# Moving the whole first map of a convolution module ahead of the depthwise convolution, and issuing the first loads from two engines

## The chip, the core and the metric

The kernel runs on one core of one Trainium2 chip. The metric is the device time of one execution in microseconds (us); three executions of the kernel before gave 954.35, 954.5 and 955.32 us, median 954.5 us. Work is shared by TensorE (PE, matrix multiplies into PSUM banks), VectorE (DVE), ScalarE (ACT), GpSimd (POOL) and SyncE (SP, which issues loads). The engines run their own instruction streams in order and wait for each other by semaphores.

## The reference

Two layers over 512 tokens of 1024 channels, float32. Only the first layer's token mixer is touched by the change:

```python
h = rmsnorm(x, norm_mix[0])
a = h @ w_pw1 + b_pw1                      # 1024 -> 2048
u = a[..., :d] * sigmoid(a[..., d:])       # gated: 1024 channels
u = causal_dwconv(u, w_dw, b_dw)           # 31 taps for each channel
u = silu(layernorm(u, ln_g, ln_b))
x = x + (u @ w_pw2 + b_pw2)
```

After it come a ConvFFN (up projection 1024 -> 5632, a convolution of width 3, gating, down projection), a pooling mixer, a second ConvFFN and a final RMSNorm.

## The kernel before, in words

Channels lie on the 128 partitions, in 8 tiles of 128 channels; tokens (512) lie along the free dimension. Each float32 operand is split in a rounded part (`_hi`) and a rest (`_lo`), and each product takes three matmul passes: hi by hi, lo by hi and hi by lo. A weight block of 128x2048 ("unit") is loaded to `w_raw[s]` by SP, rounded to `w_hi[s]` by ACT (`round_unit`, L451; the second unit of all at L492) and its rest made in `w_lo[s]` by DVE or POOL (`split_unit` L753, `split` L362). There are two slots, s = 0 and 1.

**The first map** (`w_pw1`) has four steps i = 0 to 3. Step i makes output tiles 2i and 2i+1: unit s = 0 their value half, unit s = 1 their gate half, 48 matmuls of 128x512 each. `first_unit` (L1210 to L1220) is step 0's value unit; it takes its weights in four parts and the input chunk by chunk as they land. The sum over channels for the RMSNorm (`sum_channels(0)`, L1136) is placed inside step 0's gate unit. It waits for `sumsq`: ACT squares each input tile (L470) and DVE adds them (L797). ACT takes the root (L464), DVE its reciprocal in `rms` (L772), and the results of the map are scaled by `rms` as they are drained (`scale_val` L853, `drain_gate` L859); ACT makes the sigmoid (L540), DVE multiplies value and gate (`multiply` L871).

**The depthwise convolution** is shared out. DVE makes four of the eight tiles (two pairs, `SUM_PAIRS`): per tile 31 taps, each one instruction over 512 tokens (`taps`, L841). PE makes the other four (`CONV_TILES`), each in two `conv_unit`s for 64 channels: 16 shifts by three passes of 128x256, 48 matmuls (L1165 to L1167). A conv unit's weights are blocks built from the taps, the hi block by ACT (`build_hi` L532) or POOL and the lo block by POOL (`build` L375); blocks are put in places that become free as the map ends. Its input is the gated map, rounded and rearranged by ACT (`round_even` L548, `cross_even` L555) and split by POOL (`split_even` L371). Tile 6 is shared: its first 3 shifts (6 taps) are DVE's (`shared_tap` L903, L907), and PE leaves these matmuls out. ACT drains a finished conv tile with four instructions (`drain_conv` L564).

The order is written out by hand in each engine's program. On PE it is: map steps 0, 1 and 2, conv units 0 and 1 (tile 2), map step 3, conv unit 2, a matmul for an early estimate of the channel mean (`sum_near` L1240), conv units 3 to 7. Conv unit 7 waits until tile 6 (units 4 and 5) is drained by ACT (`even_drained` at 12), since it writes the same bank. Inside unit 7, after 42 matmuls, PE makes a matmul on `rest_sum` (`sum_rest`, L1248), which DVE sums after its last tap (L923 to L934). POOL subtracts the estimated mean from the four finished tiles (L422), and ACT squares them (L603) before it drains tile 6. Then come the LayerNorm's statistics, and the second map.

**The first loads** are all issued by SP, in this order: small parameters, input tile 0, part 0 of the first unit, tile 1, tiles 2-3, part 1, tiles 4-5, parts 2 and 3, tiles 6-7, the second unit (1 MB, L320), taps, identity. An input tile is 0.25 MB (all of x 2 MB), a part 0.25 MB.

Of the kernel before, what the change touches and what calls it, by code (L numbers as in the profile page):

```python
# [81 lines left out]
CONV_TILES, SUM_PAIRS = (2, 3, 6, 7), (0, 2)  # L82
# [7 lines left out]
BUILT_BY_ACT, BUILT_BY_POOL = (0, 1, 4, 5, 7), (2, 3, 6)  # L90
# [5 lines left out]
NEAR_TILES = (0, 1, 2)  # L96
NEAR_SCALE = KD / len(NEAR_TILES)
SHARED_TILE, SHARED_SHIFTS = 6, 3
# [7 lines left out]
BANKS_PW1 = [(0, 2), (6, 0), (2, 6), (2, 6)]  # L106

BANKS_CONV = (0, 0, 1, 1, 0, 0, 1, 0)
# [6 lines left out]
def build(nc, x_in, vecs, ident_in, band_in, w_pw1, w_pw2, w_up, w_down, w_pool, out):  # L115
# [5 lines left out]
    with ctx:  # L121
# [62 lines left out]
        conv_hi = [block_hi[0], block_hi[1], block_hi[0], block_hi[1], block_hi[2], w_hi[0], w_hi[1], block_hi[3]]  # L184
        conv_lo = [block_lo[0], block_lo[1], block_lo[0], block_lo[1], block_lo[2], w_lo[0], w_lo[1], block_lo[3]]
# [38 lines left out]
        x_loaded = sems("x_loaded", 5)  # L224
# [8 lines left out]
        squared, summed = sem("squared"), sem("summed")  # L233
        stat_mm, root_done, rms_ready = sem("stat_mm"), sem("root_done"), sem("rms_ready")
# [60 lines left out]
        def _(sp):  # L295
# [30 lines left out]
            sp.wait_ge(conv_done, 5)  # L326
# [21 lines left out]
        def _(pool):  # L348
# [38 lines left out]
            pool.wait_ge(w_split[1], M_PW1 + 3)  # L387
# [3 lines left out]
            split(0, M_PW1 + 3)  # L391
            split(1, M_PW1 + 3)
            for u in (2, 3):
                pool.wait_ge(conv_done, u - 1)
                build(conv_hi, tap_hi, u).then_inc(hi_by_pool, 1)
                build(conv_lo, tap_lo, u).then_inc(lo_built, 1)
            pool.wait_ge(w_split[1], M_PW1 + PW1_STEPS)
            build(conv_lo, tap_lo, 4).then_inc(lo_built, 1)
            pool.wait_ge(unit_done[0], M_PW1 + PW1_STEPS)
            build(conv_lo, tap_lo, 5).then_inc(lo_built, 1)  # L400

# [15 lines left out]

# [3 lines left out]
            for c in range(4):  # L421
                nc.gpsimd.tensor_tensor(conv_out[:, c, :], conv_out[:, c, :], near_mean, SUB).then_inc(dev_early, 1)  # L422
# [23 lines left out]
        def _(act):  # L446
# [42 lines left out]
            square_in(0)  # L489
# [1013 lines left out]
```

## Time and profile before

| | |
|---|---|
| Times of three executions | 954.35, 954.5, 955.32 us (median 954.5) |
| The profiled execution's own time | 956.41 us |
| Its span, first to last instruction | 954.6 us |
| PE busy | 941.1 us, 99% |
| DVE, ACT, POOL busy | 555.8, 387.6, 112.2 us |
| Mean granted TensorE clock | 0.991 |

The profiled execution took 1.8 us outside its span, and 1.9 us more than the median of the runs. A PE that is shown busy may still run at half the clock, so the granted clock is read beside it. In the 40 slices of the page, PE is at nine tenths or more in all but the first and the last; DVE is as full as PE only in the first six slices (up to 143 us), where the convolution is.

### The profile page before, as it was taken

The page shows a single profiled execution, that of the slowest core. Times are in us where ns is not written, and L with a number is a line of the kernel's source. Part 1 is how long each engine was busy: PE and PEld are TensorE (multiplying, and loading weights), DVE is VectorE, ACT ScalarE, POOL GpSimd, SP SyncE. Part 2 cuts the span into 40 slices and gives each one's busy share as a digit, 9 for nine tenths or more (in the row PEclk, how much of TensorE's full clock was granted, in tenths as well). Part 3 has the DMA queues.
Part 4 walks back from the last instruction along what each step waited for, and adds up shares of the span by engine and source line. Part 5 has one row for each costly group of instructions (what it writes and reads, how often), then busy time and mean ns, then how long its engine had stood idle before and what let it go on. Part 6 is the DMA issues. An engine that isn't in the chain of part 4 may idle for free.

```text
span 954.6 us, 11837 instructions
## 1 busy us (share of the span) xinstructions
PE 941.1 (99%) x4476; PEld 791.3 (83%) x4476; DVE 555.8 (58%) x712; ACT 387.6 (41%) x593; POOL 112.2 (12%) x73
## 2 busy tenths in 40 slices
PE   8999999999999999999999999999999999999996
PEld 6889898888888888888888898888888888888886
DVE  6899995557655555555434359765555555532333
ACT  7785696344333333333223355433333333321220
POOL 0558796000000000000000020000000000000000
PEclk9999998999999999999999999999999999999998
DMA  7320022222332222322232331233222232223212
GB/s 256 111 89 1 1 90 89 89 89 88 107 114 88 88 88 88 100 92 76 78 119 91 117 134 66 89 107 113 88 88 88 88 102 91 75 90 108 91 61 88
DMA packets 17019, 88.55 MB, mean 93 GB/s; under 512 B 2016, under 2 KB 4320, under 8 KB 9952
## 3 DMA queue, kind: packets, MB, share of 16 engines
q1 hardware_dynamic: 16416, 87.67, 26.9%
q10 hardware_dynamic: 576, 0.52, 0.2%
q8 instruction: 16, 0.26, 0.1%
q14 instruction: 11, 0.09, 0.0%
HBM read 86.09 MB, written 2.10 MB: 92 GB/s over the span
## 4 chain that ended last, share of the span: by engine, by line
PE 94%; DVE 4%; DMA 1%; issue 0%; ACT 0%; SPq 0%; DVEq 0%
PE bank L1114 29%; PE bank L1116 29%; PE bank L1115 29%; DVE bank L841 2%; PE bank L1428 1%; DMA x_res<-x 1%; PE bank L1176 1%; DVE out_sb L1104 1%; PE bank L1182 0%; PE bank L1165 0%; PE bank L1166 0%; PE bank L1167 0%; PE bank L1396 0%; PE bank L1400 0%; PE bank L1401 0%
## 5 line engine op out<-in xcount | busy, mean ns | idle before, releaser
L1114 PE MATMUL bank<-h_hi,w_hi 128*128 128x512 f32 x800 | 312.3, 390 | 0.0
L1116 PE MATMUL bank<-h_hi,w_lo 128*128 128x512 f32 x800 | 311.3, 389 | 0.0
L1115 PE MATMUL bank<-h_lo,w_hi 128*128 128x512 f32 x800 | 311.2, 389 | 0.0
L451 ACT ACTIVATE w_hi<-w_raw 128x2048 fp32r<-128x2048 f32 (+2 forms) x87 | 147.3, 1693 | 211.9 <-PE bank L1116 211.8
L753 DVE TENSOR_TENSOR w_lo<-w_raw,w_hi 128x2048 fp32r<-128x2048 f32 (+2 forms) x81 | 162.2, 2002 | 100.5 <-ACT w_hi L451 99.8
L1114 PEld LDWEIGHTS bank<-h_hi,w_hi 128*128 128x128 f32 x800 | 150.2, 188 | 31.6 <-issue 0.5
L1115 PEld LDWEIGHTS bank<-h_lo,w_hi 128*128 128x128 f32 x800 | 150.2, 188 | 31.4 <-issue 0.5
L1116 PEld LDWEIGHTS bank<-h_hi,w_lo 128*128 128x128 f32 x800 | 150.2, 188 | 31.4
L1115 PE MATMUL bank<-u_lo,w_hi 128*128 128x512 f32 (+1 forms) x422 | 159.5, 378 | 0.0
L1114 PE MATMUL bank<-u_hi,w_hi 128*128 128x512 f32 (+1 forms) x374 | 141.1, 377 | 0.4 <-DVE w_lo L753 0.4
L1116 PE MATMUL bank<-u_hi,w_lo 128*128 128x512 f32 (+1 forms) x374 | 140.8, 376 | 0.0
L1115 PEld LDWEIGHTS bank<-u_lo,w_hi 128*128 128x128 f32 x422 | 79.4, 188 | 14.8
L1114 PEld LDWEIGHTS bank<-u_hi,w_hi 128*128 128x128 f32 x374 | 70.4, 188 | 13.4 <-DVE w_lo L753 0.6
L993 DVE TENSOR_TENSOR act_in<-bank,rms 128x512 f32<-128x512 f32 x44 | 28.4, 687 | 90.9 <-PE bank L1116 87.7
L1116 PEld LDWEIGHTS bank<-u_hi,w_lo 128*128 128x128 f32 x374 | 70.4, 188 | 13.0
L841 DVE SCALAR_TENSOR_TENSOR bank<-glu,par,bank 128x512 f32<-128x512 f32 x116 | 77.8, 748 | 0.0
L457 ACT ACTIVATE sq<-x_res 128x512 f32 (+1 forms) x23 | 14.5, 630 | 128.4 <-DVE x_res L1020 105.2
L666 ACT ACTIVATE u_hi<-y 128x512 f32 (+1 forms) x44 | 27.1, 633 | 89.2 <-DVE y L1008 89.2
L1008 DVE TENSOR_TENSOR y<-bank,y 128x512 f32<-128x512 f32 x44 | 28.4, 686 | 55.6 <-PE bank L1116 55.6
L662 ACT ACTIVATE y<-y 128x512 f32<-128x512 f32 x44 | 27.9, 633 | 58.4 <-DVE y L1001 57.8
L436 POOL TENSOR_TENSOR up_lo<-w_raw,up_hi 128x2048 fp32r<-128x2048 f32 x1 | 4.6, 4644 | 398.3 <-ACT up_hi L690 398.3
L1020 DVE TENSOR_TENSOR x_res<-bank,x_res 128x512 f32 (+1 forms) x15 | 10.4, 692 | 68.3 <-PE bank L1116 68.3
(195 smaller groups left out, 988.0 us busy)
## 6 DMA issues: line engine op xcount, KB each, us to landing
w_raw<-w_up SPq DMA_DIRECT2D x44, 1024.0 KB, 4.8
w_raw<-w_down SPq DMA_DIRECT2D x32, 704.0 KB, 4.1
w_raw<-w_pw SPq DMA_DIRECT2D x11, 1024.0 KB, 5.0
x_res<-x SPq DMA_DIRECT2D x3, 512.0 KB, 8.0
out<-out_sb SPq DMA_DIRECT2D x12, 128.0 KB, 1.8
w_raw<-w_pw SPq DMA_DIRECT2D x4, 256.0 KB, 7.7
w_raw<-w_pool SPq DMA_DIRECT2D x2, 512.0 KB, 3.8
band_raw<-band SPq DMA_DIRECT2D x1, 800.0 KB, 6.4
```

The source lines that it names most:

```text
L451: nc.scalar.activation(w_hi[s][:, 0:columns], w_raw[s][:, 0:columns], ACT.Copy).then_inc(w_rounded[s], 1)
L457: nc.scalar.activation(sq[:, t, :], chunk(x_res, c), ACT.Square).then_inc(squared, 1)
L662: nc.scalar.activation(y[:, t, :], y[:, t, :], ACT.Silu).then_inc(silu_done[t], 1)
L666: nc.scalar.activation(chunk(u_hi, 2 * i + t), y[:, t, :], ACT.Copy).then_inc(u_rounded[t], 1)
L753: V.tensor_tensor(w_lo[s][:, 0:columns], w_raw[s][:, 0:columns], as_f32(w_hi[s][:, 0:columns]), SUB).then_inc(w_split[s], 1)
L841: V.scalar_tensor_tensor(acc if k < TAPS - 1 else conv_out[:, c, :], src, w, acc, MUL, ADD).then_inc(tap_step[t], 1)
L993: V.tensor_tensor(act_in[:, t, 2:2 + T], bank[t][:, :], rms[:, :], MUL).then_inc(drained[t], 1)
L1008: V.tensor_tensor(y[:, t, :], bank[2 + t][:, :], y[:, t, :], MUL).then_inc(drained[2 + t], 1)
L1020: V.tensor_tensor(chunk(x_res, e), bank[t][:, :], chunk(x_res, e), ADD).then_inc(x_updated, 1)
L1114: M.matmul(dst, a, hi, start=start, stop=False)
L1115: M.matmul(dst, a, lo, start=False, stop=False)
L1116: return M.matmul(dst, b, hi, start=False, stop=stop)
```

## The change

Five things change.

1. **Order on PE.** All four steps of the map stand ahead of all conv units. DVE's four convolution tiles are now 0 to 3 (map steps 0 and 1), PE's are 4 to 7 (steps 2 and 3). Blocks, banks and the orders of ACT and POOL follow. The early mean is taken over tiles 0, 1 and 4. Tile 6 is still the shared one, with 4 shifts (8 taps) on DVE in place of 3.
2. **Step 0's gate unit** is a function of its own (`second_unit`): it starts when `w_hi[1]` is rounded, takes the passes that need only that first, and those with `w_lo[1]` later, in two groups of rows.
3. **The sum of squares** is placed after 22 of its matmuls in place of 30. ACT makes all eight squares behind the rounding of the second unit, and DVE adds them as a tree of five instructions, two of them over 1024 elements, with no cleared start.
4. **First loads.** SP issues parameters, then all of x in six loads, then the second unit. ACT issues the four parts of the first unit: two ahead of its first work, each of the others after a part is rounded.
5. **Small moves.** The pooling vectors go from DVE (after the reciprocal) to POOL (at the start); the sigmoid's table is loaded ahead of `tap_columns`, and the first sigmoid stands ahead of a rounding; the wait for the second map's loads is `conv_done` 3 in place of 5.

The first place is PE at the end of step 0's value unit and in its gate unit, before (`w_hi_69` and `w_lo_71` are the gate unit's weights; between the pieces the three passes repeat):

```order
L1220 MATMUL bank<-h_hi,w_lo_70 128x512 x2
L1114 MATMUL bank<-h_hi,w_hi_69 128x512 [waits w_split1]
L1115 MATMUL bank<-h_lo,w_hi_69 128x512
L1116 MATMUL bank<-h_hi,w_lo_71 128x512
...
L1136 MATMUL bank<-sumsq,ones 128x512 [waits summed]
L1114 MATMUL bank<-h_hi,w_hi_69 128x512
```

and now:

```order
L1228 MATMUL bank<-h_hi,w_lo_70 128x512 x2
L1239 MATMUL bank<-h_hi,w_hi_69 128x512 [waits w_rounded1]
L1240 MATMUL bank<-h_lo,w_hi_69 128x512
...
L1246 MATMUL bank<-h_hi,w_lo_71 128x512 [waits w_split1]
L1246 MATMUL bank<-h_hi,w_lo_71 128x512 x5
L1239 MATMUL bank<-h_hi,w_hi_69 128x512
...
L1141 MATMUL bank<-sumsq,ones 128x512 [waits summed]
L1239 MATMUL bank<-h_hi,w_hi_69 128x512
```

The unit no longer waits for the rest of its weights at its start, and the matmul on `sumsq` stands eight places earlier.

The second place is ACT at the same time. Before:

```order
L481 ACTIVATE w_hi_68<-w_raw_66 128x512 [waits raw_loaded0]
L475 ACTIVATE h_hi<-x_res,par 128x512 [waits x_loaded4] x2
L470 ACTIVATE in_sq<-x_res 128x512 x2
L492 ACTIVATE w_hi_69<-w_raw_67 128x2048 [waits raw_loaded1]
L470 ACTIVATE in_sq<-x_res 128x512 x6
L451 ACTIVATE w_hi_68<-w_raw_66 128x2048 [waits unit_done0,raw_loaded0]
```

and now:

```order
L467 DMA w_raw_66<-w_pw 128x512
L480 ACTIVATE h_hi<-x_res,par 128x512 [waits x_loaded3]
L480 ACTIVATE h_hi<-x_res,par 128x512 [waits x_loaded4]
L486 ACTIVATE w_hi_68<-w_raw_66 128x512 [waits part_loaded2]
L480 ACTIVATE h_hi<-x_res,par 128x512 [waits x_loaded4]
L486 ACTIVATE w_hi_68<-w_raw_66 128x512 [waits raw_loaded0]
L480 ACTIVATE h_hi<-x_res,par 128x512 [waits x_loaded5] x2
L497 ACTIVATE w_hi_69<-w_raw_67 128x2048 [waits raw_loaded1]
L475 ACTIVATE in_sq<-x_res 128x512 x8
L450 ACTIVATE w_hi_68<-w_raw_66 128x2048 [waits unit_done0,raw_loaded0]
```

All eight squares now stand behind the rounding of the gate unit's weights.

The third place is POOL from the second half of the conv inputs on (`block_hi0` and `w_hi1` are places of conv blocks, `sq` holds the near sum). Before:

```order
L371 TENSOR_TENSOR even_lo_81<-glu_even_79,even_hi_80 64x2x271 x4
L375 TENSOR_TENSOR w_hi1_69<-pair_mask_94,tap_hi_92 128x2048
L375 TENSOR_TENSOR block_lo3_89<-pair_mask_94,tap_lo_93 128x2048
L422 TENSOR_TENSOR conv_out_77<-conv_out_77,sq_74 128x512 x4
L427 TENSOR_TENSOR dev_sq_96<-dev_sq_96 128x512 x3
```

and now:

```order
L369 TENSOR_TENSOR even_lo_81<-glu_even_79,even_hi_80 64x2x271 x4
L408 TENSOR_TENSOR sq_74<-sq_74,conv_out_77 128x512
L373 TENSOR_TENSOR block_hi3_85<-pair_mask_94,tap_hi_92 128x2048
L373 TENSOR_TENSOR block_hi0_82<-pair_mask_94,tap_hi_92 128x2048
L373 TENSOR_TENSOR block_lo0_86<-pair_mask_94,tap_lo_93 128x2048
L373 TENSOR_TENSOR block_lo1_87<-pair_mask_94,tap_lo_93 128x2048
L421 TENSOR_TENSOR conv_out_77<-conv_out_77,sq_74 128x512 x4
L426 TENSOR_TENSOR dev_sq_96<-dev_sq_96 128x512 x3
```

Four builds and an addition stand between the last split of a conv input and the subtractions, in place of two builds.

The diff, cut to what the order doesn't tell:

```diff
-CONV_TILES, SUM_PAIRS = (2, 3, 6, 7), (0, 2)
+CONV_TILES, SUM_PAIRS = (4, 5, 6, 7), (0, 1)
-BUILT_BY_ACT, BUILT_BY_POOL = (0, 1, 4, 5, 7), (2, 3, 6)
+BUILT_BY_ACT, BUILT_BY_POOL = (0, 1, 2, 4, 7), (3, 5, 6)
-NEAR_TILES = (0, 1, 2)
+NEAR_TILES = (0, 1, 4)
-SHARED_TILE, SHARED_SHIFTS = 6, 3
+SHARED_TILE, SHARED_SHIFTS = 6, 4
-BANKS_CONV = (0, 0, 1, 1, 0, 0, 1, 0)
+BANKS_CONV = (6, 6, 1, 1, 0, 0, 1, 0)
 ...  # SP
-            load_x(0, 0, 1)
-            load_part(0)
-            load_x(1, 1, 2)
-            load_x(2, 2, 4)
-            load_part(1)
-            load_x(3, 4, 6)
-            load_part(2)
-            load_part(3)
-            load_x(4, 6, 8)
+            for c in range(4):
+                load_x(c, c, c + 1)
+            load_x(4, 4, 6)
+            load_x(5, 6, 8)
 ...  # ACT
+            load_part(0)
             act.wait_ge(consts_set, CONSTS)
             nc.scalar.activation(warm[:, :], eps[:, 0:1], ACT.Copy)
+            load_part(1)
 ...
                 round_part(n)
+                if n + 2 < PARTS:
+                    load_part(n + 2)
 ...  # DVE
+            def add_squares(n):
+                dve.wait_ge(squared, Q_IN + 4 * n + 4)
+                V.tensor_tensor(in_sq[:, 4 * n:4 * n + 2, :], in_sq[:, 4 * n:4 * n + 2, :], in_sq[:, 4 * n + 2:4 * n + 4, :], ADD).then_inc(in_added, 1)
+                dve.wait_ge(in_added, 2 * n + 1)
+                V.tensor_tensor(in_sq[:, 4 * n, :], in_sq[:, 4 * n, :], in_sq[:, 4 * n + 1, :], ADD).then_inc(in_added, 1)
 ...
             split_unit(1, M_PW1, UNIT)
-            for c in range(2, KD):
-                add_square(c)
+            add_squares(0)
+            add_squares(1)
+            dve.wait_ge(in_added, 4)
+            V.tensor_tensor(sumsq[:, :], in_sq[:, 0, :], in_sq[:, 4, :], ADD).then_inc(summed, KD + 1)
 ...  # PE, conv_unit
-                if n < 2:
-                    wait_drained((2, 3), DRAINED_PW1 + 2)
+                if n == 0:
+                    wait_drained((2, 3), DRAINED_PW1 + 3)
+                elif n < 3:
+                    for t in range(2):
+                        pe.wait_ge(glu_done[t], PW1_STEPS)
                 else:
-                    pe.wait_ge(even_drained, 12 if u == CONV_UNITS - 1 else 4 * (n - 2) + 4)
+                    pe.wait_ge(even_drained, 8 if g == 0 else 12)
 ...  # PE
+            def second_unit():
+                pe.wait_ge(w_rounded[1], 1)
+                for rows in ((0, 1, 2), (3, 4, 5, 6, 7)):
+                    for k in rows:
+                        for t in range(2):
+                            a, dst = w_hi[1][:, (2 * k + t) * P:(2 * k + t + 1) * P], bank[BANKS_PW1[0][1] + t][:, :]
+                            M.matmul(dst, a, h_hi[:, k, :], start=k == 0, stop=False)
+                            M.matmul(dst, a, h_lo[:, k, :], start=False, stop=False)
+                        if k == 3:
+                            sum_channels(0)
+                    pe.wait_ge(w_split[1], 1)
+                    for k in rows:
+                        for t in range(2):
+                            last = M.matmul(bank[BANKS_PW1[0][1] + t][:, :], w_lo[1][:, (2 * k + t) * P:(2 * k + t + 1) * P], h_hi[:, k, :], start=False, stop=k == KD - 1)
+                last.then_inc(unit_done[1], 1)
 ...
-                if i == 2:
-                    conv_unit(0)
-                    conv_unit(1)
+            conv_unit(0)
+            conv_unit(1)
             conv_unit(2)
             sum_near()
```

On DVE the taps are shifted between the drains: `multiply(0)` is followed by 5 taps of the first pair before `scale_val(1)`, in place of 8; the later gaps change likewise, and after `multiply(3)` 21 taps a tile are left, in place of 15. The number of DVE's own taps (31 for each of four tiles) is the same.

## Rows read from the trace of the kernel before

**Rows 1.** The page: engine, busy time, share of the span, instructions.
```profile
PE 941.1 (99%) x4476; PEld 791.3 (83%) x4476; DVE 555.8 (58%) x712; ACT 387.6 (41%) x593; POOL 112.2 (12%) x73
```

**Rows 2.** Waits of PE: waited for, us in total, times, longest.
```profile
PE bank L1210 <- ACT w_hi L481: 2.6, 2, 2.1
```

**Rows 3.** Stretches: busy (count) by engine, then PEclk, DMA share, GB/s.
```profile
12.00:13.00 1.00, 1.00 (x4) 0.87 (x3) 1.00 (x2) 1.00 (x3) 0.00 (x0) 0.53 1.06 440
200.00:400.00 200.00, 200.00 (x882) 165.29 (x881) 119.51 (x133) 75.37 (x80) 0.00 (x0) 1.00 0.28 96
```

**Rows 4.** Line L297, loads of x: ns min/median/max; then L320, second unit.
```profile
L297 SPq DMA_DIRECT2D x_res<-x x5: 425/432/1557, 1.2 to 5.5; - x5
...
DMA to landing us min/median/max: 9.5/9.5/9.5
```

**Rows 5.** Timeline of ACT: start us, us, instruction, [idle before <- releaser].
```profile
9.74 0.72 ACT L475 ACTIVATE h_hi<-x_res,par 128x512 fp32r<-128x512 f32 x1 [3.00 <-DMA x_res<-x]
16.60 1.92 ACT L492 ACTIVATE w_hi<-w_raw 128x2048 fp32r<-128x2048 f32 x1
18.43 3.21 ACT L470 ACTIVATE in_sq<-x_res 128x512 f32<-128x512 f32 x6
```

**Rows 6.** Timeline of DVE at the start of the map.
```profile
18.56 2.29 DVE L753 TENSOR_TENSOR w_lo<-w_raw,w_hi 128x2048 fp32r<-128x2048 f32 x1 [0.72 <-ACT w_hi L492]
20.77 4.66 DVE L797 TENSOR_TENSOR sumsq<-sumsq,in_sq 128x512 f32<-128x512 f32 x6
...
37.58 1.41 DVE L871 SCALAR_TENSOR_TENSOR glu<-bank,par,act_in 128x512 f32<-128x512 f32 x2 [1.72 <-ACT act_in L540]
```

**Rows 7.** Timeline of PE: first matmul, start of the gate unit, the sum.
```profile
6.09 0.47 PE L1210 MATMUL bank<-h_hi,w_hi 128*128 128x512 f32 x1 [0.46 <-ACT w_hi L481]
...
21.03 0.40 PE L1114 MATMUL bank<-h_hi,w_hi 128*128 128x512 f32 x1
...
27.85 1.02 PE L1136 MATMUL bank<-sumsq,ones 128*128 128x512 f32 x2
...
28.93 0.39 PE L1115 MATMUL bank<-h_lo,w_hi 128*128 128x512 f32 x1
```

**Rows 8.** Timeline of PE in the convolution: unit 2, near sum, unit 7, rest sum.
```profile
109.61 0.28 PE L1165 MATMUL bank<-even_hi,block_hi 128*128 128x256 f32 x1
...
115.30 1.02 PE L1240 MATMUL bank<-sq,mean_w 128*128 128x512 f32 x2
...
137.02 0.36 PE L1165 MATMUL bank<-even_hi,block_hi 128*128 128x256 f32 x1
...
143.12 0.67 PE L1248 MATMUL bank<-sq,mean_w 128*128 128x512 f32 x1 [0.86 <-DVE sq L934]
```

**Rows 9.** Timeline of POOL: a split, builds, conv input splits, subtractions.
```profile
38.26 4.63 POOL L362 TENSOR_TENSOR w_lo<-w_raw,w_hi 128x2048 fp32r<-128x2048 f32 x1
...
93.94 7.22 POOL L375 TENSOR_TENSOR block_lo<-pair_mask,tap_lo 128x2048 fp32r<-128x2048 f32 x2
...
115.61 5.79 POOL L371 TENSOR_TENSOR even_lo<-glu_even,even_hi 64x542 fp32r<-64x542 f32 x4 [2.06 <-issue]
...
125.06 4.08 POOL L375 TENSOR_TENSOR block_lo<-pair_mask,tap_lo 128x2048 fp32r<-128x2048 f32 x1
129.10 5.06 POOL L422 TENSOR_TENSOR conv_out<-conv_out,sq 128x512 f32<-128x512 f32 x4
```

**Rows 10.** Timeline of ACT: the drain of tile 6 and what follows.
```profile
134.85 0.49 ACT L564 ACTIVATE conv_out<-bank,par 64x256 f32<-64x256 f32 x1
...
136.90 1.92 ACT L451 ACTIVATE w_hi<-w_raw 128x2048 fp32r<-128x2048 f32 x1
```

**Rows 11.** Timeline of DVE: two shared taps, end of the rest sum.
```profile
124.18 1.48 DVE L903 SCALAR_TENSOR_TENSOR bank<-glu_even,par,sq 128x512 f32<-128x512 f32 x1
...
126.89 0.74 DVE L907 SCALAR_TENSOR_TENSOR bank<-glu_even,par,bank 128x512 f32<-128x512 f32 x1
...
142.28 0.69 DVE L934 TENSOR_TENSOR sq<-bank,conv_out 128x512 f32<-128x512 f32 x1
```

More of the change, by code:

```diff
@@ L324, in _ @@
                 load_step(w_pw1, 2 * i, M_PW1 + i, UNIT)
-            sp.wait_ge(conv_done, 5)
+            sp.wait_ge(conv_done, 3)
             with sp.Fori(0, PW2_STEPS) as i:
@@ L386, in _ @@
             split(1, M_PW1 + 2)
-            pool.wait_ge(w_split[1], M_PW1 + 3)
+            split(0, M_PW1 + 3)
+            split(1, M_PW1 + 3)
             split_even(0)
@@ L390, in _ @@
             pool.wait_ge(even_split, 4)
[L391 to L398, printed above, removed]
+            for t in range(2):
+                pool.wait_ge(w_split[t], M_PW1 + PW1_STEPS)
+            build(conv_lo, tap_lo, 2).then_inc(lo_built, 1)
             pool.wait_ge(unit_done[0], M_PW1 + PW1_STEPS)
-            build(conv_lo, tap_lo, 5).then_inc(lo_built, 1)
+            build(conv_hi, tap_hi, 3).then_inc(hi_by_pool, 1)
+            build(conv_lo, tap_lo, 3).then_inc(lo_built, 1)
             for t in range(2):
@@ L414, in _ @@
             pool.wait_ge(even_split, 8)
+            pool.wait_ge(even_drained, 4)
+            pool.wait_ge(near_added, 1)
+            nc.gpsimd.tensor_tensor(near_sum, near_sum, conv_out[:, NEAR_TILES[2], :], ADD).then_inc(near_added, 1)
+            build(conv_hi, tap_hi, 5).then_inc(hi_by_pool, 1)
+            pool.wait_ge(conv_done, 1)
+            pool.wait_ge(lo_built, 6)
             build(conv_hi, tap_hi, 6).then_inc(hi_by_pool, 1)
+            build(conv_lo, tap_lo, 6).then_inc(lo_built, 1)
+            pool.wait_ge(conv_done, 2)
             build(conv_lo, tap_lo, 7).then_inc(lo_built, 1)
+            pool.wait_ge(near_added, 2)
             pool.wait_ge(near_copied, 1)
             pool.wait_ge(even_drained, 8)
-            for c in range(4):
+            for c in EARLY_TILES:
                 nc.gpsimd.tensor_tensor(conv_out[:, c, :], conv_out[:, c, :], near_mean, SUB).then_inc(dev_early, 1)
@@ L603, in square_dev @@
                 nc.scalar.activation(dst[rows, :], conv_out[rows, c, :], ACT.Square).then_inc(dev_squared, 1)
-            for c in range(4):
-                act.wait_ge(dev_early, c + 1)
-                square_dev(c, dev_sq[:, c, :])
+            for n, c in enumerate(EARLY_TILES):
+                act.wait_ge(dev_early, n + 1)
+                square_dev(c, dev_sq[:, n, :])
             drain_conv(2)
@@ L875, in _ @@
             multiply(0)
-            taps(0, 0, 8)
+            taps(0, 0, 5)
             scale_val(1)
-            taps(0, 8, 13)
+            taps(0, 5, 13)
             drain_gate(1)
@@ L929, in _ @@
             dve.wait_ge(dev_late, 1)
-            V.tensor_scalar(rest, conv_out[:, 4, :], 1.0, None, MUL).then_inc(rest_added, 1)
-            for n, c in enumerate((5, 6, 3)):
+            V.tensor_scalar(rest, conv_out[:, LATE_TILES[0], :], 1.0, None, MUL).then_inc(rest_added, 1)
+            for n, c in enumerate((LATE_TILES[1], LATE_TILES[2], EARLY_TILES[3])):
                 dve.wait_ge(rest_added, n + 1)
```

123 lines of the change are left out of this document (59 added, 64 removed).

## The prediction

> **What bounds the kernel now.** I read the page first: PE is busy for 941.1 of 954.6 us [rows 1], and the chain of waits runs almost wholly on it. So only three things can move the end: matmuls taken away, time in which PE waits, and time in which it runs at the lower clock. Next the waits of PE: outside the last stage they are few and all lie before 150 us, in the stretch that the change rewrites. Then the stretches: with the clock granted in full, 200 us hold 882 matmuls of 512 columns, 0.227 us each, so a unit of 48 takes 10.9 us [rows 3]. Last the timelines of the first 30 us and of 110 to 143 us.
>
> At the start PE does its first unit from 6.09 to 21.03 us [rows 7], 14.9 us for work of 10.9. 2.1 us of the loss is one wait [rows 2]: ACT sat idle for 3.0 us until input tiles 2-3 landed at 9.7 [rows 5]. After this wait the granted clock fell: 0.53 in the stretch 12 to 13 us, the lower of TensorE's two levels, 1.2 for 2.4 GHz [rows 3]. That is the other 1.9 us. The gate unit then ran from 21.03 with the sum in it at 27.85, after 30 matmuls, and no wait, since `sumsq` was ready at 20.77 + 4.66 = 25.43 [rows 6, 7]. From 28.93, 17 more matmuls make its end 28.93 + 17 x 0.227 = 32.8 us; from the sum's start to the unit's end are 4.95 us, of which 18 matmuls take 4.08, so the sum costs 0.87. Call the end of the gate unit E; before, E = 32.8.
>
> At the end of the convolution PE's `sum_rest` starts at 143.12, E + 110.3, after a wait of 0.86 us on DVE's sum, which ended at 142.97 [rows 8, 11]. Unit 7 started at 137.02, right after ACT had drained tile 6 at 136.9 [rows 8, 10]. So three queues, PE, DVE and ACT (behind POOL), meet here within a microsecond. Everything behind 143.12 is the same program before and after; a shift there is a shift of the end.
>
> **First part: E after the change.** PE's matmuls up to E are the same number. What decides is a chain that the new order tightens. Call R the time at which the gate unit's weights are rounded (before: 16.60 + 1.92 = 18.52, right at their landing [rows 5]). Behind R, ACT makes all eight squares: six took 3.21, so eight take 4.3 and end at R + 4.2 (each starts a little inside the one before). DVE splits for 2.3 us [rows 6], adds the first four squares, and then must have the eighth: from R + 4.3 it makes one addition over 1024 elements and two over 512. An addition over 512 takes 4.66 / 6 = 0.78 with its turnaround [rows 6]; over 1024 no row shows one; it lies between 0.78 (were length free) and 1.56 (two of them), and a split of 2048 in 2.29 puts it at 1.2 to 1.3, which I take. The sum is ready at R + 4.3 + 1.3 + 1.55, about R + 7.2. PE comes to it 22 matmuls, 5.0 us, after the start of the gate unit, which cannot start before R. So PE arrives at R + 5.1 if R is late and waits 2.1 us for a sum that it did not wait for before. From the sum's start 26 matmuls are left: 26 x 0.227 + 0.87 = 6.8. Hence E = R + 14.0 (R + 7.2 + 6.8), or, if the first unit's own end F is later than R + 2.2, E = F + 5.0 + 6.8 = F + 11.8.
>
> F: PE starts at about 6.1 as before. Input tile 2 is now a load of 0.25 MB of its own, and part 1 does not stand behind it on SP. If both land by 8.5, the 2.1 us wait and the low clock are gone and F = 6.1 + 10.9 = 17.0; if the wait is a microsecond, 18. Then E is set by R for every R above 15.
>
> R: the weights landed 9.5 us after their issue at 7.1 [rows 4, 5]. An issue costs SP 0.43 us, but the last load of x held it for 1.56 [rows 4]. With the parts gone from SP, the gate unit's is the sixth issue behind that of input tile 0 at 1.2 [rows 4], and goes out at about 3.9. But the bytes ahead of its last byte stay the same, all 2 MB of x, 1 MB of parts (ACT's four loads run beside) and its own 1 MB, and the DMA engines are already full, at 440 GB/s, in 12 to 13 us [rows 3]. So the bounds of the landing are 16.6 (nothing gained but the issue) and 4.3 MB at 440 GB/s from 2 us on, 11.8. Most of the stretch is bound by bytes, so I stay near the row and take 15.4: R = 17.3 and E = 31.3, 1.5 us earlier than before.
>
> The Trainium skill speaks against the loads' part. DMA: Bandwidth & Descriptors, section "Issuing engines are not separate DMA queues", says that loads issued by different engines run on the same 16 DMA engines and interleave, and that one saves only the issuing time. The trace has one issuing engine at the start, so no row bears it out; by it the landing is that of the third rival below.
>
> **Second part: from E to the rest sum.** The map's steps 1 to 3 run through: six units, 65.3 us. Their waits are all covered: DVE's drains and multiplies fall before PE needs their banks, and POOL's splits of 4.63 [rows 9] end 1 us or more ahead of their units, as before. Then unit 0 to 7 of the convolution. A unit took 109.61 to 115.30, 5.7 us for 48 matmuls [rows 8]; units 4 and 5 now have 36 (4.3 us), 0.7 us less in all than with 39. PE alone: E + 65.3, three units to 82.5, the near sum (0.9 with its turnaround) behind a wait of 0.3 for POOL's addition to 83.7, unit 3 to 89.4, units 4 and 5 to 98.0, unit 6 to 103.7.
>
> POOL, in order, all after E: its last split ends at 43.5 (four units) + 1.9 + 4.6 = 50.2; four conv input splits 5.8, to 56.4; three builds of 3.6 to 67.2; an addition (1.3, as a subtraction [rows 9]) to 68.5; two builds to 75.7; four input splits to 81.5; an addition to 82.8; four builds to 97.2; four subtractions, 5.1, to 102.3. ACT makes the last square, then drains tile 6 in 2.05 (134.85 to 136.90 [rows 10]; the drain began 0.7 after the last subtraction): 105.0. Tile 6's drain was late by 0.1 us before; now PE is at unit 7 at 103.7 and waits 1.3. What is more, DVE's first shared tap now falls at E + 97.4, on the subtractions: before, this tap took 1.48 for 0.74 and POOL's build beside it 4.08 for 3.61 [rows 9, 11]. That puts 0.2 to 0.5 on the drain, 105.2. 42 matmuls (5.0) later PE is at the rest sum: E + 110.2.
>
> The Trainium skill explains these two rows: SBUF — State Buffer, section "Who interferes with whom", says that an elementwise instruction of VectorE with both inputs in SBUF keeps GpSimd's reads out. The rows agree; the cost above is from the rows.
>
> DVE: from the end of its first multiply (37.58 + 1.41 = 39.0) to 142.97 it took 104.0, waits included [rows 6, 11]. Two more shared taps of 0.74 make 105.5; the first multiply ends 3.1 after E (a drain, a sigmoid and two multiplies, with the table now loaded before). DVE is ready at E + 108.6, 1.6 before PE: its wait is gone, and the queue of POOL and ACT is late in its place. So the two savings here, 0.86 of wait and 0.7 of matmuls, are given back: E + 110.2 against E + 110.3.
>
> **The sum.** Profiled: 956.4 - (32.8 - 31.3) - 0.1 = 954.8. That execution took 1.9 us more than the median of the runs, so in their terms 954.5 - 1.6 = 952.9. At nothing I cost the pooling vectors on POOL (it has nothing else to do until the taps are rounded), the earlier `conv_done` (those loads are needed 20 us later), and ACT's issues (the sequencer's, beside 0.6 us roundings). If the cover of the last goes, four times 0.43 us, 1.7, delay R by as much, and E too.
>
> **Rivals.**
> - *The clock falls in the gate unit.* PE waits 2.1 us for the sum, as long as the wait after which it fell at 12 us, and for one spell like that one (1.9 us lost) E becomes 33.2: 954.8. For: the same length of wait. Against: the fall at 12 us is the only case of such a length in the trace, and conv matmuls go on at the full rate after the waits of 0.2 and 0.9 us at 137 and 143. With R no earlier than before it ends on the slower side: E = 18.5 + 14.0 + 1.9 = 34.4, 956.0. It decides from R = 17.0 on (17.0 + 14.0 + 1.9 = 32.9). Chance 0.22, half of it above 954.5.
> - *No wait: the loads come early.* R at or below 15, F = 17.0: E = 28.8, 950.4; if POOL's queue is also a microsecond shorter than summed, 949.4. For: the part of 1.56 us in which SP was held. Against: the DMA engines' full row. Chance 0.22.
> - *The loads gain nothing.* R = 18.5, E = 32.5: 954.1, no change to be measured. Chance 0.11.
> - *POOL's queue is longer than summed.* Each 3.6 us build that slips puts its slip on unit 7 at once; a slip of 3.5 us makes 956.4. For: 20 instructions in a row without a gap. Against: two builds in a row take 7.22 [rows 9], and nothing slips there before. Chance 0.05.
>
> **Numbers.** My forecast, 952.9, has 0.4, its own range 951.8 to 954.0. A change of 0.2% is 1.9 us, about what can be told from none: faster is below 952.6, slower above 956.4. Faster holds the second rival (0.22) and not quite half of the forecast, where R earlier by 0.4 us is enough (0.18): 0.4. Slower: the far end of the first rival, with a second spell at the lower clock, and half of the last, 0.08. Same: 0.52. Range 949.9 to 955.9.
>
> **What would show it.** In the profile after: the granted clock at 12 to 16 us at its upper level and the gate unit starting at 17 to 18; a wait of PE on DVE at the sum, about 2 us, and the clock behind it; the map's end at E + 65.3; a wait of PE on ACT's drain at unit 7 of 1 to 2 us and none on the rest sum. I am wrong if the gate unit's weights are rounded before 16 us (then well below 952), if the clock falls behind the sum, or if unit 7 does not wait (then up to 1.5 us lower).

## The result, and the profile after

The changed kernel takes 958.58 us, the kernel before 954.78 us in runs beside it (medians of seven each): a ratio of 1.0033 with a 95% interval of 1.0023 to 1.0043. It is slower, by 0.2 to 0.4%, where 952.9 was forecast and slower had 0.08. The profiled execution of the changed kernel took the median itself, 958.58, with a span of 956.6. Of all the runs of this document one, a run of e8 below (1180.2 us at a mean granted clock of 0.751), fell into a slow state and is left out of the ratios.

The page's busy line is that of before [rows 1] within a tenth for PE and DVE, with the six matmuls fewer (x4470 for x4476):

```profile
PE 941.0 (98%) x4470; PEld 789.5 (83%) x4470; DVE 555.7 (58%) x705; ACT 387.7 (41%) x594; POOL 112.9 (12%) x78
```

The waits of PE, in the columns of [rows 2]. The 2.1 us for part 1 is gone, and these five rows stand in its place (0.4 of the 0.8 is the wait ahead of the very first matmul, 0.5 before):

```profile
PE bank L1218 <- ACT h_hi L480: 1.6, 2, 1.1
...
PE bank L1173 <- ACT conv_out L569: 1.5, 1, 1.5
PE bank L1141 <- DVE sumsq L821: 1.0, 1, 1.0
PE bank L1218 <- ACT w_hi L486: 0.8, 2, 0.4
PE bank L1261 <- POOL sq L408: 0.6, 1, 0.6
```

The granted clock in two stretches, in the columns of [rows 3]: at 12 us it no longer falls, and the DMA engines move the same 440 GB/s; at 18 us PE waits for its first unit's last rows.

```profile
12.00:13.00 1.00, 1.00 (x6) 0.87 (x5) 1.00 (x2) 0.40 (x1) 0.00 (x0) 1.00 1.06 440
18.00:19.00 1.00, 0.88 (x3) 0.44 (x4) 1.00 (x3) 1.00 (x2) 0.00 (x0) 1.00 0.00 0
```

The loads. First the four parts, now issued by ACT (ns of an issue, then us to landing), then the gate unit's from SP, which answer to [rows 4]:

```profile
L467 ACTq DMA_DIRECT2D w_raw<-w_pw x4: 335/349/418, 0.7 to 9.8; - x4
...
DMA to landing us min/median/max: 3.4/7.2/8.1
```

```profile
L313 SPq DMA_DIRECT2D w_raw<-w_pw x1: 1832/1832/1832, 4.1 to 4.1; - x1
...
DMA to landing us min/median/max: 12.4/12.4/12.4
```

The gate unit's load goes out 3.0 us earlier, at 4.1 for 7.09, and lands at 4.1 + 12.4 = 16.5, as before. The last part goes out at 9.8. It stands behind the rounding of part 1 in the order, but it leaves 0.6 us before that rounding starts: what held it were ACT's waits for input tiles 0 to 2, the last of which had landed by 9.75. ACT's timeline shows this and what follows (the columns of [rows 5]):

```profile
9.75 0.72 ACT L480 ACTIVATE h_hi<-x_res,par 128x512 fp32r<-128x512 f32 x1 [1.08 <-DMA x_res<-x]
9.76 0.34 ACTq L467 DMA_DIRECT2D w_raw<-w_pw  x1
10.38 0.62 ACT L486 ACTIVATE w_hi<-w_raw 128x512 fp32r<-128x512 f32 x1
...
16.71 0.63 ACT L486 ACTIVATE w_hi<-w_raw 128x512 fp32r<-128x512 f32 x1 [2.37 <-DMA w_raw<-w_pw]
17.24 1.32 ACT L480 ACTIVATE h_hi<-x_res,par 128x512 fp32r<-128x512 f32 x2
18.47 1.90 ACT L497 ACTIVATE w_hi<-w_raw 128x2048 fp32r<-128x2048 f32 x1
20.27 4.26 ACT L475 ACTIVATE in_sq<-x_res 128x512 f32<-128x512 f32 x8
```

ACT stands for 2.37 us until part 3 lands at 16.7, rounds it and tiles 6 and 7, and only then rounds the gate unit's weights, landed since 16.5: R, their rounding's end, is 20.37, against 18.52 before and 17.3 forecast. DVE's additions, which answer to [rows 6], take 1.22 over 1024 elements and end at 27.31, R + 6.9:

```profile
22.61 1.22 DVE L801 TENSOR_TENSOR in_sq<-in_sq 128x1024 f32<-128x1024 f32 x1
...
26.62 0.69 DVE L821 TENSOR_TENSOR sumsq<-in_sq 128x512 f32<-128x512 f32 x1
```

PE (see [rows 7 and 8]): a wait in the first unit, the gate unit from 21.25, the sum behind a wait, then the near sum, unit 7 and the rest sum:

```profile
18.00 0.74 PE L1218 MATMUL bank<-h_hi,w_hi 128*128 128x512 f32 x2 [1.13 <-ACT h_hi L480]
...
21.25 0.39 PE L1239 MATMUL bank<-h_hi,w_hi 128*128 128x512 f32 x1
...
27.37 1.12 PE L1141 MATMUL bank<-sumsq,ones 128*128 128x512 f32 x2 [0.97 <-DVE sumsq L821]
...
117.41 1.13 PE L1261 MATMUL bank<-sq,mean_w 128*128 128x512 f32 x2 [0.57 <-POOL sq L408]
...
140.02 0.36 PE L1173 MATMUL bank<-even_hi,block_hi 128*128 128x256 f32 x1 [1.45 <-ACT conv_out L569]
...
145.12 0.59 PE L1269 MATMUL bank<-sq,mean_w 128*128 128x512 f32 x1
```

With the 6.8 us from the sum's start to the unit's end, E, the gate unit's end, is 27.37 + 6.8 = 34.2 (before 32.8), and the rest sum comes at E + 110.9 (before E + 110.3). DVE's first shared tap and POOL's builds beside it, POOL and ACT ahead of unit 7, and DVE's rest sum, which is no longer waited for [rows 9 to 11]:

```profile
119.87 1.63 DVE L907 SCALAR_TENSOR_TENSOR bank<-glu_even,par,sq 128x512 f32<-128x512 f32 x1
```

```profile
117.32 7.66 POOL L373 TENSOR_TENSOR block_hi<-pair_mask,tap_hi 128x2048 fp32r<-128x2048 f32 x2
124.94 7.21 POOL L373 TENSOR_TENSOR block_lo<-pair_mask,tap_lo 128x2048 fp32r<-128x2048 f32 x2
132.11 5.05 POOL L421 TENSOR_TENSOR conv_out<-conv_out,sq 128x512 f32<-128x512 f32 x4
```

```profile
137.85 0.50 ACT L569 ACTIVATE conv_out<-bank,par 64x256 f32<-64x256 f32 x1
...
139.90 1.92 ACT L450 ACTIVATE w_hi<-w_raw 128x2048 fp32r<-128x2048 f32 x1
```

```profile
142.70 0.69 DVE L939 TENSOR_TENSOR sq<-bank,conv_out 128x512 f32<-128x512 f32 x1
```

From 143.12 to 145.12 is 2.0 us, and 2.0 is the difference of the spans; another 0.2 lies outside the span (2.0 us for 1.8). The medians differ by 3.8 since the profiled execution of before was slower than its median by 1.6; the experiments come back to that.

### The profile page after: what moved, and what is told of

It reads as the page before. It is cut to its first block, busy times and chain, and to the rows that moved or that the text cites. A ratio compares the mean times of both kernels' runs of the same rounds, so it can differ in the third digit from the quotient of the medians.

```text
span 956.6 us, 11821 instructions
## 1 busy us (share of the span) xinstructions
PE 941.0 (98%) x4470; PEld 789.5 (83%) x4470; DVE 555.7 (58%) x705; ACT 387.7 (41%) x594; POOL 112.9 (12%) x78
## 4 chain that ended last, share of the span: by engine, by line
PE 86%; DVE 7%; POOL 3%; DMA 2%; ACT 1%; issue 1%; SPq 0%; DVEq 0%; POOLq 0%
PE bank L1119 26%; PE bank L1121 26%; PE bank L1120 26%; DVE bank L845 4%; POOL block_lo L373 1%; PE bank L1449 1%; POOL block_hi L373 1%; DMA x_res<-x 1%; DMA w_raw<-w_pw 1%; PE bank L1184 1%; DVE out_sb L1109 1%; POOL even_lo L369 1%; POOL conv_out L421 1%; PE bank L1190 0%; DVE w_lo L759 0%
## 5 line engine op out<-in xcount | busy, mean ns | idle before, releaser
L1119 PE MATMUL bank<-h_hi,w_hi 128*128 128x512 f32 x784 | 305.7, 390 | 0.0
L1121 PE MATMUL bank<-h_hi,w_lo 128*128 128x512 f32 x784 | 305.1, 389 | 0.0
L1120 PE MATMUL bank<-h_lo,w_hi 128*128 128x512 f32 x784 | 305.1, 389 | 0.0
L1121 PEld LDWEIGHTS bank<-h_hi,w_lo 128*128 128x128 f32 x784 | 147.2, 188 | 30.7
L1120 PEld LDWEIGHTS bank<-h_lo,w_hi 128*128 128x128 f32 x784 | 147.2, 188 | 30.7 <-issue 0.2
L1119 PEld LDWEIGHTS bank<-h_hi,w_hi 128*128 128x128 f32 x784 | 147.2, 188 | 30.6 <-issue 0.2
```

The lines of the kernel that those rows point to most:

```text
L1119: M.matmul(dst, a, hi, start=start, stop=False)
L1120: M.matmul(dst, a, lo, start=False, stop=False)
L1121: return M.matmul(dst, b, hi, start=False, stop=stop)
```

## The experiments

In this table R (the gate unit's weights rounded), F (start of the gate unit), E and the rest sum are read from each profiled execution, E as the sum's start plus 6.8 us where 22 matmuls stand ahead of it, plus 4.95 where 30 do. They are one execution each. The ratio is to the kernel before in runs on the same chip, with its interval. The experiments were run in three sets, in which the kernel before had medians of 955.82, 955.86 and 955.86 us over 96 runs, 1.1 more than in the first set; so ratios, not medians, are compared with the changed kernel's.

| kernel | R | F | E | rest sum | median us | ratio |
|---|---|---|---|---|---|---|
| before | 18.5 | 21.0 | 32.8 | E + 110.3 | 954.78 | 1 |
| changed | 20.4 | 21.3 | 34.2 | E + 110.9 | 958.58 | 1.0033 (1.0023 to 1.0043) |
| e1 before again | 18.7 | 21.3 | 33.0 | E + 110.3 | 956.00 | 1.0002 (0.9993 to 1.0010) |
| e2 changed, loads of before | 18.4 | 18.8 | 32.2 | E + 110.9 | 956.47 | 1.0003 (0.9994 to 1.0012) |
| e3 before, new loads | 21.5 | 23.9 | 37.4 | E + 110.3 | 959.52 | 1.0036 (1.0023 to 1.0049) |
| e4 changed, parts at once | 16.6 | 20.3 | 32.1 | E + 110.8 | 955.82 | 0.9997 (0.9988 to 1.0006) |
| e5 = e4, drain first | 17.8 | 19.9 | 31.7 | E + 109.2 | 953.43 | 0.9970 (0.9960 to 0.9980) |
| e6 = e4, three shifts | 17.6 | 19.7 | 31.5 | E + 110.9 | 956.03 | 0.9998 (0.9989 to 1.0007) |
| e7 changed, sum later | 20.2 | 21.1 | 32.9 | E + 111.8 | 958.08 | 1.0024 (1.0014 to 1.0034) |
| e8 before, parts at once | 18.8 | 21.2 | 33.0 | E + 110.3 | 955.71 | 0.9995 (0.9986 to 1.0005) |
| e9 = e5, three shifts | 17.1 | 19.7 | 31.5 | E + 109.8 | 954.47 | 0.9990 (0.9981 to 0.9999) |
| e10 changed, part 3 late | 19.2 | 20.1 | 33.0 | E + 110.9 | 956.72 | 1.0012 (1.0003 to 1.0021) |
| e11 = e5, parts behind warm-up | 17.7 | 19.2 | 31.5 | E + 109.3 | 953.62 | 0.9980 (0.9971 to 0.9988) |
| e12 = e2, drain first | 18.3 | 19.3 | 32.1 | E + 109.3 | 954.50 | 0.9984 (0.9974 to 0.9993) |

**The kernel before again** (no edit).

> The kernel before, unchanged, for the clock of each of its runs. Theory A: the fall of the granted clock at 12 to 15.5 us, which the profile of before shows, is an accident of that one execution. Then the runs at 954.5 have a mean clock of 0.993, a run at 956.4 has 0.991, and a profile without the fall has E (end of the gate unit) at 30.9 in place of 32.8. Rival B: every execution has the fall, and 956.4 against 954.5 is scatter from elsewhere; then all runs have 0.991 and E is 32.8 each time.

Its profile has the fall again, at 12.5 us, E 33.0 and a mean clock of 0.991. Of the 29 runs of before that were measured beside it one other has 0.991 (956.57); the eight from 954.25 to 955.00 have 0.995 or 0.996. So neither theory stands as written: the fall is no accident of one profile, but most runs have a higher mean clock. What is shown is that the scatter goes with the clock: in the last set of 35 runs those at 0.996 lie between 953.4 and 955.3, the five at 0.991 between 956.3 and 958.1. In e1's own set this is looser: three runs at 0.993 (957.08 to 957.57) are slower than both at 0.991 (956.43 and 956.57). A mean clock does not tell which stretch was at the lower level.

**The loads alone, both ways.** In the changed kernel the loads go back to SP:

```diff
-            for c in range(4):
-                load_x(c, c, c + 1)
...
+            load_x(0, 0, 1)
+            load_part(0)
+            load_x(1, 1, 2)
...
+            load_part(3)
+            load_x(4, 6, 8)
```

> The changed kernel with the first loads issued as before: all by SP, in the old order, tiles 2-3 as one load; everything else is as changed. Theory A: R (gate unit's weights rounded) went from 18.5 to 20.4 because part 3 was issued late by ACT; so R comes back to 18.5, the wait for the sum is 1 to 2 us, E is 32.5 to 32.8 instead of 34.3, and the time 957.0 (956.6 to 957.4). Rival B: R is bound by bytes alone, or by ACT's queue of roundings; then R stays at 20.4 and the time at 958.6.

and in the kernel before they go to the two engines, in ACT's loop:

```diff
+            load_part(0)
+            load_part(1)
...
                 round_part(n)
+                if n + 2 < PARTS:
+                    load_part(n + 2)
```

> The kernel before with only the two-engine loads of the change (SP issues x and the rest, ACT the four parts); squares, sums and the convolution stay as before. Theory A: R becomes 20.4, PE's gate unit starts at 21.2 and has no wait for the sum (six squares behind R: ready at 27.3, PE there at 28.0), so E is 33.0. Against a run of before without the clock's fall (E = 30.9) that is 2.1 us: 956.7; against one with it 0.3: 955.0. Rival B: the loads are innocent, R stays at 18.5 and the time at 954.7 or less, since the clock no longer falls.

Without the new loads the changed kernel has no loss (1.0003), and with them alone the kernel before has one as large as that of the whole change (1.0036). R returned to 18.4, right behind the landing:

```profile
16.46 1.92 ACT L498 ACTIVATE w_hi<-w_raw 128x2048 fp32r<-128x2048 f32 x1 [1.14 <-DMA w_raw<-w_pw]
```

The wait for the sum stayed, 1.4 us. E was 32.2, a little below the 32.5 to 32.8 of theory A. The time gained more than A had: 957.0 stood for 2.2 us above before's median of the first set, and measured are 0.7 above that of this set. In the kernel before the loads did more harm than forecast, E 37.4 for 33.0. Two squares stand there ahead of the gate unit's rounding, so that R is 21.5, and PE waits for DVE's split of it too, 2.4 us, after which the clock fell once:

```profile
23.92 0.50 PE L1113 MATMUL bank<-h_hi,w_hi 128*128 128x512 f32 x1 [2.37 <-DVE w_lo L752]
```

```profile
24.00:28.00 4.00, 4.00 (x11) 3.14 (x12) 3.48 (x6) 3.75 (x4) 0.00 (x0) 0.57 0.76 246
```

The difference in E to the changed kernel is 3.2 us. In it are the wait for the split, which the changed kernel's `second_unit` doesn't have since it starts on the rounded half alone, the later R, and this fall of the clock; no run takes them apart.

**When the parts are issued.** The changed kernel with all four at ACT's start:

```diff
-            load_part(0)
+            for n in range(PARTS):
+                load_part(n)
...
-            load_part(1)
...
-                if n + 2 < PARTS:
-                    load_part(n + 2)
```

> The changed kernel with all four parts issued by ACT at its start, one behind the other, none behind a rounding. Theory A (late issue of part 3 costs the time): part 3 lands by 13.5, ACT rounds it and tiles 6 and 7 before the second unit lands at 16.5, R is 18.4, E 32.4 to 32.6, time 956.8. Rival B: the parts' bytes now push the input tiles back, PE starts or runs its first unit a microsecond or two later, and what R gains is lost there: 958 to 959.

Theory A holds in its cause, and the gain is larger than its 956.8: even the gate unit's load lands earlier, at 14.65. R is 16.6, the wait for the sum is gone, and 3.6 thousandths of the time come back.

```profile
14.68 1.92 ACT L495 ACTIVATE w_hi<-w_raw 128x2048 fp32r<-128x2048 f32 x1
```

The stretches fit this: with late parts the DMA engines moved less from 5 to 9 us, and were busy for 0.73 of the first two of these microseconds, against 0.94. First the changed kernel, then this one (last column GB/s):

```profile
5.00:7.00 2.00, 1.61 (x7) 1.25 (x6) 1.27 (x2) 1.12 (x2) 0.00 (x0) 1.00 0.73 225
7.00:9.00 2.00, 1.55 (x7) 1.00 (x6) 0.32 (x2) 0.72 (x1) 0.00 (x0) 1.00 0.94 257
```

```profile
5.00:7.00 2.00, 0.88 (x5) 0.58 (x3) 0.36 (x1) 1.22 (x2) 0.17 (x1) 1.00 0.94 321
7.00:9.00 2.00, 1.84 (x4) 1.49 (x5) 1.37 (x3) 0.74 (x2) 0.00 (x0) 1.00 1.05 404
```

The same edit in the kernel before:

> The kernel before with two-engine loads, but the four parts issued at ACT's start one behind the other. Theory A: the two engines were no loss by themselves, only the late issue of parts 2 and 3 was. All the loads land 2 us earlier than from SP alone (the gate unit's at 14.7, not 16.6), R is 17 to 17.8, no wait lies ahead of the gate unit, and E is 30.9 to 32 as the clock at the start allows (the kernel before: 31.1 without the clock's fall, 33.0 with it): 954.5 to 955.5, the same as before within 0.1%, and 4 us less than with the late issue. Rival B: the input tiles come later beside the parts and PE loses more than a microsecond: 956.5 or more.

The ratio is as A had it, no gain and 4 us less than with late parts. The positions are not: R is 18.8, not 17.0 to 17.8, since two squares stand ahead of it, PE waits 0.9 us for the split, and E is 33.0 for 30.9 to 32. This profile has no fall of the clock at the start, and its E and rest sum (143.35) are still those of e1 (143.31), which has one. Next, parts 0 to 2 at once and only the last part late:

```diff
-                if n + 2 < PARTS:
-                    load_part(n + 2)
+                if n == 1:
+                    load_part(PARTS - 1)
```

> The changed kernel with parts 0 to 2 issued at ACT's start and only part 3 left behind the rounding of part 1. Theory A: the late issue of the last part alone makes the loss: it goes out at about 10 and lands at 16 to 16.7, R is 19.5 to 20.3, E 33.5 to 34.2, 957.5 to 958.5, as in the changed kernel. Rival B: the loss came from all the late parts together, or with more bytes moved early part 3 lands within 4 us of its issue (14 or before): R 17 to 18, E 32, 955.5 to 956.

Neither theory holds; it lies between the two. Part 3 goes out at 9.2 and lands at 15.5, E is 33.0, between e4's 32.1 and 34.2, and the ratio 1.0012 lies between 0.9997 and 1.0033. Its interval overlaps that of e4 and ends just below that of the changed kernel, so how much the last part alone makes is told by the positions, 0.9 of 2.1 us, and not by the times.

```profile
15.56 0.63 ACT L486 ACTIVATE w_hi<-w_raw 128x512 fp32r<-128x512 f32 x1 [2.60 <-DMA w_raw<-w_pw]
17.33 1.90 ACT L497 ACTIVATE w_hi<-w_raw 128x2048 fp32r<-128x2048 f32 x1
```

**The wait for the sum.** One number in `second_unit`, `if k == 3` to `if k == 5`.

> The changed kernel, its loads as they are, with PE's sum of the squares placed behind 30 matmuls of the gate unit (where it stood before), not 22. Theory A: R is 20.4 as in the changed kernel; PE comes to the sum at 28.1, when it has been ready since 27.3, the wait of 1.1 us is gone and E is 33.1 in place of 34.2: 957.5. Rival B: the wait for the sum costs nothing because what DVE does behind it (the reciprocal of 3.3 us, the drains) decides later on: then the rest sum stays at 145.1 and the time at 958.6.

E is 32.9, as A had it (33.1), but of the 1.3 us 0.9 come back, 0.7 of it at once as a new wait. The root behind the sum is ahead of ACT's tap columns and of POOL's first build; all of them start 0.46 us later than in the changed kernel, and POOL's next split is then late for step 1's gate unit:

```profile
44.62 0.47 PE L1119 MATMUL bank<-h_hi,w_hi 128*128 128x512 f32 x1 [0.67 <-POOL w_lo L360]
```

The rest sum came 0.4 us earlier and the ratio is 1.0024 for 1.0033, too near to tell apart. The sum's place is a balance of two waits.

**The wait ahead of unit 7.** On top of the parts at once, ACT's `drain_conv(2)` is moved ahead of the four squares:

```diff
+            drain_conv(2)
             for n, c in enumerate(EARLY_TILES):
                 act.wait_ge(dev_early, n + 1)
                 square_dev(c, dev_sq[:, n, :])
-            drain_conv(2)
```

> The changed kernel with all four parts issued at ACT's start (as in the run before), and besides ACT's drain of tile 6 put ahead of the four squares of the early tiles. Theory A: PE's wait of 1.7 us ahead of unit 7 is a wait for that drain, which stands behind POOL's four subtractions in ACT's order; with the drain first the wait is gone, the rest sum is then bound by DVE's sum, and comes 109.2 us behind the gate unit's end E in place of 110.8; 1.5 us off the time of the version with the parts at once. Rival B: the squares, now later, or DVE's sum take the wait's place, and the rest sum stays at E + 110.5 or more; no gain.

The drain now starts as unit 5 ends, at 130.34, and not behind POOL; PE has no wait and is at the rest sum at 140.88:

```profile
130.34 0.49 ACT L567 ACTIVATE conv_out<-bank,par 64x256 f32<-64x256 f32 x1 [2.60 <-PE bank L1173]
...
132.40 1.68 ACT L607 ACTIVATE dev_sq<-conv_out 128x512 f32<-128x512 f32 x3
```

```profile
140.88 1.02 PE L1267 MATMUL bank<-sq,mean_w 128*128 128x512 f32 x2
```

That is E + 109.2, to the tenth, but not for A's reason: DVE's sum was ready at 140.2, before PE came to it, so what is left is PE's own work. At 0.9970 this version beats both kernels. Then the shared shifts, `SHARED_SHIFTS = 3` for 4, with the wait and without it:

> The changed kernel with the parts at once, and with three shifts of tile 6 computed by DVE for PE as before, not four: PE's units 4 and 5 have 39 matmuls each in place of 36, 0.7 us more. Theory A: the 0.7 us is taken out of the wait ahead of unit 7 (1.7 becomes 1.0), the rest sum stays at E + 110.8, the time is the same. Rival B: the matmuls count, or DVE with two instructions less lets the drain come earlier: the rest sum moves by 0.7 us to the later side, or by up to 1.5 us to the earlier.

> As e5_once_drain_first (parts at once, drain of tile 6 ahead of the squares), but with three shifts of tile 6 shared in place of four. Theory A: with the wait ahead of unit 7 gone, nothing covers the 6 matmuls (0.7 us) any more: the rest sum comes at E + 110.3 instead of 109.6, and the median is 0.7 us above that of e5 (0.9978 of before against 0.997). Rival B: the rest sum is still set by DVE or ACT; then it stays at E + 109.6 or, since DVE has two instructions less, comes earlier.

With the wait in place the 0.7 us of matmuls came out of it: 0.8 us was left of 1.4, the rest sum at E + 110.9, the time the same.

```profile
PE bank L1171 <- ACT conv_out L567: 0.8, 1, 0.8
```

Without it the rest sum moved from E + 109.2 to E + 109.8 (A had the step, 0.7, and its ends 0.5 too late), and the median in its own set was 0.85 us above e11's, whose loads differ a little:

```profile
141.34 1.02 PE L1267 MATMUL bank<-sq,mean_w 128*128 128x512 f32 x2
```

So the fourth shift is worth its 0.7 us only once the queue behind it is cleared. Last, two variants of the loads with the drain moved:

> As e5_once_drain_first, but with parts 1 to 3 issued behind ACT's warm-up (from 2.1 us on), so that input tiles 0 and 1 stand before them. Theory A: E is there set by PE's first unit, which started at 7.5 for want of tile 0; now it starts at 6.3 and ends earlier by up to 1.2 us, while R stays at 17 to 18: E 30.5 to 31.5, the median 952.5 to 953.4. Rival B: what tiles 0 and 1 gain the later tiles or the gate unit's load lose, E stays at 31.7 or above: 953.4 to 954.

> The changed kernel with the old loads (SP alone) and the drain of tile 6 ahead of the squares. Theory A: R 18.4, the wait for the sum about 1 us or hidden by a low clock, E 32.2 to 32.5, the rest sum at E + 109.6: 1.3 us below the version with the old loads alone, about 954.6, and 0.5 to 1 us above e5. Rival B: the loads at once bring nothing at all, and the two versions measure the same, 953.4.

e11's gate unit starts at 19.2 and E is 31.5, at the end of A's range, but the time is rival B's, 953.62. e12 is at 954.50, as A had it, 0.9 us above e11 by the medians and 0.6 by E, with ratios whose intervals overlap. So what two engines with every load issued at the start are worth is not told apart from nothing; by the medians it is about 0.9 us.

## Why the prediction was wrong

From 952.9 to 958.6 are 5.7 us. They are 2.9 in E, 0.7 from E to the rest sum, 1.9 in the last line of the sum, and 0.2 outside the span.

- *R, the step that failed.* The prediction had the gate unit's weights landed at 15.4 and rounded at 17.3, and costed ACT's issues at nothing but the sequencer's 0.43 us each. What they cost is where they stand. Parts 2 and 3 stood in ACT's order behind waits for input tiles, and went out at 4.9 and 9.8; the last took 6.9 us more to land. Before, SP had issued it at 4.5. ACT works in order, so the gate unit's rounding stood behind part 3's. R came 3.1 us later than forecast: 1.1 because the gate unit's weights landed at 16.5, and 2.0 because ACT was still at part 3 and tiles 6 and 7 until 18.5. Against before it is 1.9 later. The "sixth issue" was reckoned rightly (4.1 for 3.9) and gained nothing, as the third rival had it. The Trainium skill (DMA: Bandwidth & Descriptors, section "Issuing engines are not separate DMA queues") says that loads from several engines share the same 16 DMA engines and that only the time of issuing is saved. The row agrees: 3.0 us earlier out, 0.1 us earlier in. By itself the rule would have given 954.1. With all issued at the start, the gate unit's weights landed between 14.7 and 16.0 (e4, e5, e8, e9, e11), around the 15.4 that was forecast.
- *E = R + 14.0* held: 13.8 in the changed kernel, e2, e10, e11 and e12, whatever R was; and where R was early, E = F + 11.8 held in e4 to e6 and e9. The addition over 1024 took 1.22 (forecast 1.2 to 1.3). F was wrong, 21.3 for 17 to 18: the first unit waited 1.13 us at 18.0 for tile 6, which ACT rounds behind part 3, and before that 0.45 and 0.36 us at 8.7 and 11.1. At 8.7 and 18.0 the next pass then stood about 0.4 us more, until DVE had split the same tile. In no profile was F below 18.8, so R = 17.3 alone would not have made E = 31.3. The 2.1 us wait and the fall at 12 us did go; the time was waited for elsewhere.
- *The clock behind the sum* did not fall: the granted clock is 1.00 from the start to 150.5 us. The first rival's condition did not arise: the wait was 1.0 us, not 2.1, since PE too was late. The longest wait there, 1.4 us in e2, brought no fall either.
- *From E to the rest sum* the mechanism was right and its size 0.7 us short. The near sum waited 0.6 for POOL (forecast 0.3), POOL's queue ended at E + 103.0 (forecast 102.3, though the items of that sum make 101.7). About 0.4 us of it is the tap beside POOL: it came at 119.87, E + 85.7, where the forecast had E + 97.4, and fell on a build (two took 7.66, the next two 7.21) and not on the subtractions, which took 5.05 as before. So unit 7 waited 1.45 for ACT's drain (forecast 1.3) on a PE that was itself later. DVE's wait is gone, and e6 and e9 show that the 0.7 us of matmuls were given back there, as forecast.
- *The last line of the sum.* The profiled sum was 956.4 - 1.6 = 954.8, and then 1.9 was taken off because that execution was slower than the median. The sum had already taken out the clock's fall, worth 1.9 us. If the median runs were faster because they don't have it, it was counted twice, and by its own steps the forecast should have been 954.8, no change. That they don't have it is not shown. What is shown is that the 1.9 was no fixed property of that profile: it rested on three runs, was 1.6 against seven, and e1's profile, with the same fall, was 0.6 above the median of the runs beside it.

So of the 3.8 us between the two medians 2.0 are seen between the profiles, and 0.2 outside the spans. The other 1.6 stay open. Without the fall before would have E = 30.9 (32.8 - 1.9), and 3.3 in E and 0.6 behind it would make 3.9. In favour of this are e2 and e12, which have the old loads and no fall, and that few runs of before are at 0.991. Against it is e8: it has no fall, its E is 33.0, and its ratio is 0.9995; were most runs of before at E = 30.9, e8 should be about 2 us slower than they are. The stretches at the lower clock behind 145 us, told of below, are worth about 1 us and are in the medians too.

## What to carry to other kernels

An issue written into a compute engine's order is worth as much as what stands ahead of it: put all loads that are already allowed ahead of the engine's first wait, and ask of each one what the engine must wait for before it can issue. When a profiled execution is slower than the median, find out what made it so before the difference is subtracted: it may be an event that the sum has already taken out, or the scatter of three runs. A wait that takes up a saving shows where the next edit is: here one line, a drain moved ahead of four squares, was worth 1.6 us and made the saved matmuls count. The largest part of the change, the new order on PE, was never run by itself; what it is worth stays open.

## What the runs showed of the hardware

- Which stretches are at the lower clock differs between executions of nearly the same program. Between 145 and 158 us it was 6.8 us in seven profiles and 3.4 in seven; another stretch, of about 3 to 8 us, lies in the last ten. From the rest sum to the end of the span took 811.0 to 811.7 us with 6.8, and 809.9 to 810.7 with 3.4. That is as large as most effects here. In e1 and e8 the rest sum comes at the same time, and the profiled executions differ by 1.2 us (956.43 and 955.25). That is why each effect above is read from a position in the trace and not from the median alone.
- In e3, e4, e9, e11 and e12 PE's first matmuls were 0.43 us apart, not 0.23, until 10 to 11 us, in e4 until 11.6, behind the same 16 small matmuls as in the others. That is the spacing of the stretch at 13 us in the kernel before, where the granted clock is 0.50; but here the column of the granted clock reads 1.00, so it doesn't show the lower level, and the cause stays open. It cost e4 some 2 us: F was 20.3 though R was 16.6. In its timeline a pair takes 1.05 us, and in the changed kernel's row below it 0.61:

```profile
9.00 1.05 PE L1226 MATMUL bank<-h_hi,w_lo 128*128 128x512 f32 x2
```

```profile
7.66 0.61 PE L1228 MATMUL bank<-h_hi,w_lo 128*128 128x512 f32 x2
```

- A load issued while many bytes are under way takes longer: parts issued at 9.2 to 9.9 us took 6.4 to 6.9 us for 0.25 MB; those issued at 0.7, with hardly anything ahead of them, took 3.4 to 4.2.
